# Second mixer: index key and index weights in one weight tile, seventeen tiles in place of eighteen

## What is computed

```python
q, k, v, qi, ki, wi = split(h @ w_in)          # 1024, 256, 256, 512, 64, 8 columns
q = _rope(_rmsnorm(q, q_norm_g), positions)
k = _rope(_rmsnorm(k, k_norm_g), positions)
qi = _rope(qi, positions)                      # 8 index heads of 64
ki = _rope(_layernorm(ki, idx_k_ln_g, idx_k_ln_b), positions)   # one index key head
wi = wi * (IDX_HEADS ** -0.5 * IDX_DIM ** -0.5)
# per block of 128 queries:
s = einsum('bqhd,bsd->bqhs', qib, ki)
score = einsum('bqhs,bqh->bqs', relu(s), wib)  # causal
_, sel = top_k(score, 128)                     # then attention over the selected keys
```

## Time and profile before

| | |
|---|---|
| time, median of 3 | 2121.99 us (2121.92 to 2122.03) |
| the profiled execution's own time | 2123.01 us |
| its span | 2120.9 us |
| PE, PEld busy | 99%, 81% |
| DVE, ACT, POOL busy | 58%, 37%, 14% |
| the chain that ended last | PE 91%, DVE 6%, ACT 1% |
| second mixer's tiles from index 3 to the attention | about 954 to 1063 us |
| its attention | about 1063 to 1171 us |

### The profile page before, as it was taken

One profiled execution on the slowest core, in us unless ns is written; L12 is line 12 of the kernel. 1 busy time (PEld: TensorE's weight loads), 2 busy tenths in 40 slices (PEclk: granted clock), 3 DMA queues, 4 the chain that ended last, 5 costly groups with the idle time before them and its releaser, 6 DMA issues.

```text
span 2120.9 us, 28344 instructions
## 1 busy us (share of the span) xinstructions
PE 2101.8 (99%) x10024; PEld 1725.9 (81%) x10024; DVE 1239.1 (58%) x1832; ACT 782.3 (37%) x1081; POOL 299.9 (14%) x357
## 2 busy tenths in 40 slices
PE   9999999999999999999999999999999999999999
PEld 8888888887888888877767788888888878888887
DVE  7666544786576654466995576654465456333332
ACT  6222333557432223344364432223343224222222
POOL 0122401650212240024300212210000000000000
PEclk9999999999999999999999999999999999999999
DMA  5566233320355632323300345542333222222232
GB/s 193 179 199 198 88 106 112 124 86 1 109 169 189 198 126 84 100 87 115 115 16 1 110 150 197 190 139 82 95 99 110 100 80 100 90 98 99 76 95 87
DMA packets 79572, 243.33 MB, mean 115 GB/s; under 512 B 12784, under 2 KB 13424, under 8 KB 79376
## 3 DMA queue, kind: packets, MB, share of 16 engines
q1 hardware_dynamic: 61376, 189.61, 27.3%
q0 software_dynamic: 18128, 52.84, 8.0%
HBM read 235.84 MB, written 2.29 MB: 112 GB/s over the span
## 4 chain that ended last, share of the span: by engine, by line
PE 91%; DVE 6%; ACT 1%; issue 1%; POOL 1%; DMA 0%; SPq 0%; ACTq 0%; DVEq 0%; POOLq 0%
PE ps L709 28%; PE ps L711 28%; PE ps L710 28%; PE ps L1016 2%; PE ps L974 1%; PE ps L995 1%; DVE tmp L1627 1%; DVE ps L1973 1%; DVE small L1868 1%; PE ps L977 0%; PE ps L1142 0%; DVE w_lo L1584 0%; ACT w_hi L1225 0%; POOL w_lo L618 0%; PE ps L743 0%
## 5 line engine op out<-in xcount | busy, mean ns | idle before, releaser
L709 PE MATMUL ps<-h_hi,w_hi 128*128 128x512 f32 x1888 | 740.1, 392 | 1.5 <-DVE h_lo L1913 0.9
L711 PE MATMUL ps<-h_hi,w_lo 128*128 128x512 f32 x1888 | 735.0, 389 | 0.0
L710 PE MATMUL ps<-h_lo,w_hi 128*128 128x512 f32 x1888 | 734.8, 389 | 0.0
L1584 DVE TENSOR_TENSOR w_lo<-w_raw,w_hi 128x1024 fp32r<-128x1024 f32 x336 | 411.4, 1226 | 381.3 <-ACT w_hi L1225 367.7
L1225 ACT ACTIVATE w_hi<-w_raw 128x1024 fp32r<-128x1024 f32 x383 | 402.2, 1052 | 242.0 <-PE ps L711 240.2
L709 PEld LDWEIGHTS ps<-h_hi,w_hi 128*128 128x128 f32 x1888 | 353.6, 187 | 82.2 <-issue 7.5
L711 PEld LDWEIGHTS ps<-h_hi,w_lo 128*128 128x128 f32 x1888 | 353.6, 187 | 75.2
L710 PEld LDWEIGHTS ps<-h_lo,w_hi 128*128 128x128 f32 x1888 | 353.7, 187 | 73.0 <-issue 0.2
L710 PE MATMUL ps<-hid_lo,w_hi 128*128 128x512 f32 x704 | 273.9, 389 | 0.0
L711 PE MATMUL ps<-hid_hi,w_lo 128*128 128x512 f32 x704 | 273.9, 389 | 0.0
L709 PE MATMUL ps<-hid_hi,w_hi 128*128 128x512 f32 x704 | 273.9, 389 | 0.0
(11 more groups left out here) (308 smaller groups left out, 1778.0 us busy)
## 6 DMA issues: line engine op xcount, KB each, us to landing
ada_raw<-in_ada_w POOLq DMA_DIRECT2D x96, 512.0 KB, 4.8
w_raw<-in_gate SPq DMA_DIRECT2D x88, 512.0 KB, 3.8
w_raw<-in_up SPq DMA_DIRECT2D x88, 512.0 KB, 3.5
w_raw<-in_down SPq DMA_DIRECT2D x64, 384.0 KB, 3.0
w_raw<-in_down SPq DMA_DIRECT2D x64, 320.0 KB, 2.8
w_raw<-in_w_mix_c SPq DMA_DIRECT2D x24, 512.0 KB, 3.4
w_raw<-in_w_mix_b SPq DMA_DIRECT2D x17, 512.0 KB, 3.5
w_raw<-in_w_mix SPq DMA_DIRECT2D x16, 512.0 KB, 3.5
```

What stands on the lines that cost most here:

```text
L709: pe.matmul(dest, s_hi, m_hi, start=first and n == 0, stop=False)
L710: pe.matmul(dest, s_hi, m_lo, start=False, stop=False)
L711: mm = pe.matmul(dest, s_lo, m_hi, start=False, stop=last and n == len(pairs) - 1)
L1584: dve.tensor_tensor(chunk(w_lo, slot, WT), chunk(w_raw, slot, WT), f32(chunk(w_hi, slot, WT)), ALU.subtract).then_inc(w_lo_done, 1)
```

## The change

The index key's 64 columns and the 8 index weights are put into one tile (the rest of it is zero), so there are seventeen tiles. The second tile of `first_two` is now `qi0`: DVE multiplies it by the rstd and ACT adds its shift. The key is made once, in the lower 64 partitions; a fifth DMA copies it to the upper ones, and the rope of the key waits for it. As the list is one shorter, what hangs on a tile's place moves: the loads with their swaps, POOL's waits, the ropes, the index slots (two chunks earlier), the rounds in `TOPS_AT` (32 early ones in place of 33), and the key's spread (from `betweenB(5, 0)` to `betweenB(4, 1)`).

```diff
                    "mk0", "mk1", "mv0", "mv1"]
-        TILES_B = ["ki", "wi", "qi0", "qi1", "qi2", "qi3", "vB0", "vB1", "kB0", "kB1"] + [f"qB{t}" for t in range(8)]
+        TILES_B = ["ki", "qi0", "qi1", "qi2", "qi3", "vB0", "vB1", "kB0", "kB1"] + [f"qB{t}" for t in range(8)]
         first_job, at = {}, 0
...
         def shift_sum(n, s):
-            return tmp[:, 3 * T + s * P:3 * T + s * P + (8 if n == 3 and s == 1 else P)]
+            return tmp[:, 3 * T + s * P:3 * T + (s + 1) * P]
 
...
             if t == "ki":
-                return 6
+                return 5
             at = (TILES_A if t in TILES_A else TILES_B).index(t)
...
                 return rot_ring[n % 2 + (0 if t in TILES_A else 2)], 64 * (n // 2 + 1)
-            return rot_key[t], 64
+            return rot_key[t], 80 if t == "ki" else 64
 
...
         ROUND_LIST = [(b, r) for b in range(1, TT) for r in range(ROUNDS)]
-        TOPS_AT = {8: (0, 1), 9: (4, 1), 10: (5, 2), 11: (4, 1), 12: (0, 2), 13: (3, 0), 14: (3, 0), 15: (3, 0), 16: (3, 0),
-                   17: (1, 0)}
+        TOPS_AT = {8: (1, 4), 9: (1, 5), 10: (2, 4), 11: (1, 0), 12: (2, 0), 13: (3, 0), 14: (3, 0), 15: (3, 0), 16: (3, 0)}
         TOP_EARLY = sum(before + between for before, between in TOPS_AT.values())
...
 
-            at = 4 * (m - 6) + 2 * part - 2
-            return IDX[max(at, 0):at + 2] if 0 <= at < len(IDX) else []
+            at = 4 * (m - 6) + 2 * part
+            return IDX[at:at + 2] if 0 <= at < len(IDX) else []
 
...
                         after(sp, h_sin, "ki")
+                if t == "ki":
+                    sp.dma_start(kraw[HD:P, :], kraw[0:HD, :]).then_inc(rot_sem(t)[0], 16)
                 half = 8 if t in TILES_A else HD // 2
                 for head in range(0, P, HD):
                     for to, of in ((head, head + half), (head + half, head)):
+                        of = of % HD if t == "ki" else of
                         sp.dma_start(turned(t)[to:to + half, :], straight(t)[of:of + half, :]).then_inc(rot_sem(t)[0], 16)
 
             def mixer(tiles, mix, last, weights):
                 J = first_job[mix]
                 for j in range(len(tiles) + KC):
                     if j < len(tiles):
-                        width = KC * 8 if tiles[j] == "wi" else WT
                         if tiles is TILES_B and j in (4, 5):
                             after(sp, shift_acc, (3, j - 4, KC - 1))
-                        load(J + j, 0, 4, A[weights][j, :, 0:width])
+                        load(J + j, 0, 4, A[weights][j])
                     else:
                         load(J + j, 0, 4, A[WEIGHTS[last]][j - len(tiles)])
-                    due = [t for t in tiles if has_rope(t) and j == tiles.index(t) + {"q": 7, "k": 10 if t == "ki" else 9}[t[0]]]
+                    due = [t for t in tiles if has_rope(t) and j == tiles.index(t) + {"q": 7, "k": 9}[t[0]]]
                     for t in sorted(due, key=lambda t: t[0] == "k"):
...
             for j in range(LEAD, len(TILES_B) + KC):
+                if j == 8:
+                    after(pool, h_roped, "qi3")
                 if j == 9:
-                    after(pool, h_roped, "qi3")
+                    after(pool, i_sum, (1, 5))
                 if j == 10:
-                    after(pool, i_sum, (1, 5))
-                if j == 11:
                     after(pool, i_sum, (2, 1))
-                if 15 <= j <= 20:
-                    after(pool, h_roped, f"qB{j - 15}")
+                if 14 <= j <= 19:
+                    after(pool, h_roped, f"qB{j - 14}")
                 split(first_job["mixB"] + j)
...
                         for s in range(2 * pair, 2 * pair + 2):
-                            width = 8 if n == 3 and s == 1 else P
-                            mm = product(None, bank(s)[0:width, :], [(weights(js + s, k, width),
-                                                                       (chunk(hi, k), chunk(lo, k)))], k == 0, k == KC - 1)
+                            mm = product(None, bank(s), [(weights(js + s, k), (chunk(hi, k), chunk(lo, k)))],
+                                         k == 0, k == KC - 1)
                             if k == KC - 1:
...
                 for b in range(MT if t[:2] == "mk" else TT):
-                    for half in range(2):
+                    for half in range(1 if t == "ki" else 2):
                         mm = pe.matmul(bank(5)[half * HD:(half + 1) * HD, b * P:(b + 1) * P],
...
                     after(pe, h_roped, "ki")
+                    after(pe, v_done, "wi")
                 if pair[0][0] == 1:
...
 
-                if part == 0 and m == 5:
+                if part == 1 and m == 4:
                     head_spread("ki")
-                if part == 0 and TILES_B[m - 2] in h_normed.value and m > 4:
+                if part == 0 and TILES_B[m - 2] in h_normed.value and m > 2:
                     head_spread(TILES_B[m - 2])
                 if part == 0 and m == 3:
                     after(pe, evac, "ki")
-                    pe.matmul(bank(6), matsB[:, P:2 * P], kraw[:, :], start=True, stop=True)\
+                    pe.matmul(bank(6)[0:HD, :], matsB[0:HD, P:P + HD], kraw[0:HD, :], start=True, stop=True)\
                         .then_inc(p_misc.at("ki_total"), 1)
                 if part == 1 and m == 3:
-                    turn_tile(TILES_B, 1)
-                if part == 0 and is_token_major(TILES_B[m - 1]) and m > 2:
-                    turn_tile(TILES_B, m - 1)
+                    turn_tile("wi")
+                if part == 0 and is_token_major(TILES_B[m - 1]):
+                    turn_tile(TILES_B[m - 1])
                 if part == 0 and has_norm(TILES_B[m - 1]):
...
             after(act, d_misc, "ki_scaled")
-            act.activation(kraw[:, :], kraw[:, :], ACT.Identity, bias=shift_out(3, 0)).then_inc(evac.at("ki"), 1)
+            act.activation(kraw[0:HD, :], kraw[0:HD, :], ACT.Identity, bias=shift_out(3, 0)[0:HD, :])\
+                .then_inc(evac.at("ki"), 1)
+            after(act, d_misc, "wi_scaled")
+            act.activation(features_of("wi"), features_of("wi"), ACT.Identity, bias=shift_out(3, 0)[HD:HD + 8, :])\
+                .then_inc(evac.at("wi"), 1)
             lead(J + 1)
             for m in range(2, len(TILES_B) + 1):
                 t = TILES_B[m - 1]
                 act.wait_ge(job_done, J + m + RING)
                 if has_norm(t):
                     head_square(t, hsB)
-                if t[:2] in ("qB", "qi"):
+                if t == "qi0":
+                    after(act, d_misc, "qi_scaled")
+                    act.activation(straight(t), straight(t), ACT.Identity, bias=shift_out(3, 1)).then_inc(h_scaled.at(t), 1)
+                elif t[:2] in ("qB", "qi"):
                     head_scale(t, col("g_q2") if t[:2] == "qB" else 1.0, straight(t))
                 elif t[:2] == "kB":
                     head_gain(t, col("g_k2"), straight(t))
-                elif t == "wi":
-                    after(act, d_misc, "wi_scaled")
-                    act.activation(features_of(t), features_of(t), ACT.Identity, bias=shift_out(3, 1)[0:8, :])\
-                        .then_inc(evac.at(t), 1)
                 else:
                     act.activation(features_of(t), tile_bank(t), ACT.Copy).then_inc(evac.at(t), 1)
                 if m < len(TILES_B):
                     lead(J + m)
                 if m == 3:
                     after(act, d_misc, "ki_ctr")
-                    head_square("ki", hsB, src=kraw[:, :])
+                    head_square("ki", hsB, src=kraw[0:HD, :])
                 if m == 3:
-                    keep_tile("wi", 1, wi[:, :], WI_SCALE)
+                    keep_tile("wi", 0, wi[:, :], WI_SCALE)
                 if t[:2] == "vB":
...
                 after_nth(dve, h_roped, before)
+                if t == "ki":
+                    dve.wait_ge(*rot_sem(t))
                 dve.tensor_tensor(chunk(rop, 0), straight(t), tab_cos, ALU.mult)
...
             dve.wait_ge(job_done, J + 2 + RING)
-            dve.tensor_tensor(kraw[:, :], bank(0), ssum[:, :], ALU.mult).then_inc(d_misc.at("ki_scaled"), 1)
-            dve.tensor_tensor(relu[0:8, 0:T], bank(1)[0:8, :], ssum[0:8, :], ALU.mult).then_inc(d_misc.at("wi_scaled"), 1)
+            dve.tensor_tensor(kraw[0:HD, :], bank(0)[0:HD, :], ssum[0:HD, :], ALU.mult).then_inc(d_misc.at("ki_scaled"), 1)
+            dve.tensor_tensor(features_of("wi"), bank(0)[HD:HD + 8, :], ssum[HD:HD + 8, :], ALU.mult)\
+                .then_inc(d_misc.at("wi_scaled"), 1)
+            dve.tensor_tensor(straight("qi0"), bank(1), ssum[:, :], ALU.mult).then_inc(d_misc.at("qi_scaled"), 1)
 
...
                     after(dve, p_misc, "ki_total")
-                    dve.scalar_tensor_tensor(kraw[:, :], bank(6), -1.0 / HD, kraw[:, :], ALU.mult, ALU.add)\
+                    dve.scalar_tensor_tensor(kraw[0:HD, :], bank(6)[0:HD, :], -1.0 / HD, kraw[0:HD, :], ALU.mult, ALU.add)\
```

(11 more changed lines are left out.)

40 lines of the change are left out of this document (20 added, 20 removed).

## The result

After the change the kernel takes 2136.77 us (median of 6 runs, 2132.67 to 2145.39), and the kernel before, run beside it, 2123.39 us (6 runs, 2121.92 to 2126.48). The ratio is 1.0062, with a 95% interval of 1.0047 to 1.0077. Slower was predicted; 2130.7 us was not, and 2136.77 lies 2.8 us above the range. The profiled execution took 2137.41 us, its span is 2135.6 us.

A forecast was written before the change was run, and what follows sets the result against it. PE (99% busy) was taken to bound the kernel, with helpers it waits for: -5.95 + 0.75 + 5.4 + 1.65 + 1.5 + 2.15 + 2.9 + 0.3 = +8.7 us, giving a median of 2130.7 us; range 2121 to 2134.

The forecast's parts named there:

- The tile: Second mixer: one tile less on PE saves 5.44 us, the key's smaller rstd spread 0.5: gain 5.95 us.
- The start: Stage's start: PE waits longer for DVE's shift sum, now 128 columns wide: +0.75 us, bounds 0.5 and 1.1.
- Stall A: At the index key's spread PE waits for DVE's reciprocal behind qi1's rope: +5.4 us, lower bound 3.4.
- Stall B: At the turn of vB1 PE waits for ScalarE's evacuation behind relu 3: +1.65 us, range 0.6 to 1.7.
- rival (c): PE's clock halves after a stall, hidden after A, not after E: +1.4 us; chance of over 2134 us 0.07.
- C: Index loop, kB0's spread: its rstd comes behind sums 10, 11 and four rounds: +1.5 us, range 0.3 to 1.5.
- D: Index loop, kB1's spread: its rstd comes late behind five rounds on DVE: +2.15 us, bounds 1.5 and 2.5.
- E: Index loop, qB2's head sum: its squares wait behind relus 22, 23, sums and ropes: +2.9 us, lower 1.2.
- The attention: Its first scores wait for DVE, which ends the tile loop about 0.3 us further behind PE: +0.3 us.

The follow-up runs named there:

- e12: e10 with DVE's ropes of kB0 and kB1 behind the sums of their step, two rounds moved behind them, one fewer in the loop; 2126.94 us, 1.0001.
- e11: The kernel before with its second tile 128 columns wide, 8 of them used (wide load, sum and matmuls); 2127.28 us, ratio 1.0018.
- e5: The changed kernel with small unread matmuls ahead of the waits at the spreads of the key, kB0 and kB1; 2134.85 us, ratio 1.0052.
- e2: The changed kernel with the index key's std on ACT and its reciprocal on DVE taken earlier; 2137.26 us, ratio 1.0065.
- e4: The changed kernel with only DVE's reciprocals of kB0 and kB1 earlier, ahead of the second slot's rounds and sums; 2134.60 us, ratio 1.0059.
- e7: e3 and e4 joined, plus DVE's norms of kB0 and kB1 ahead of the second slot's rounds; 2132.05 us, ratio 1.0043.
- e1: The changed kernel with only the key's spread put back to its old place, chunk 2 of tile 5; 2137.49 us, ratio 1.0057.
- e3: e2 plus DVE's norm of the key ahead of the rope of qi1, so its swap comes earlier; 2130.47 us, ratio 1.0036.
- e8: The changed kernel with the index slots and the distribution of rounds as before the change, nothing else; 2135.37 us, ratio 1.0049.
- e9: e7 with the index slots and rounds as before the change; 2128.85 us, ratio 1.0020.
- e10: e9 with PE's product of the shift sums moved behind the stage's first six matmuls; 2127.30 us, ratio 1.0009.
- e13: e12 with small unread matmuls: 3 ahead of the last head sum, 9 in place of 5 behind the attention's second scores; 2123.94 us, 1.0001.
- e14: The kernel before with only PE's product of the shift sums moved behind the stage's first six matmuls; 2122.48 us, ratio 0.9989.

## Why the prediction was right in sign and too small

- **The tile, -5.95: 1.0 too much.** e12's loop is 5.4 us shorter than before's with no new wait in it, 0.4 of it from the start; so the change is worth 5.0. The pitch of the tile, 5.44, was right, but the spread of the key's rstd is no shorter for having 8 matmuls in place of 16: 1.02 us from its start to the next matmul in e12, and 1.03 before. The key's sum, now made in 64 partitions only, keeps PE for 1.00 us in place of 0.46. The first fence is before, the second e12:

```profile
954.64 1.02 PE L1153 MATMUL ps<-kraw,matsB 128*128 128x512 f32 x2
955.10 0.80 PE L709 MATMUL ps<-h_hi,w_hi 128*128 128x512 f32 x1
...
969.02 0.50 PE L709 MATMUL ps<-h_hi,w_hi 128*128 128x512 f32 x1
```
```profile
955.28 1.07 PE L1165 MATMUL ps<-kraw,matsB 64*64 64x512 f32 x2
956.28 0.50 PE L712 MATMUL ps<-h_hi,w_hi 128*128 128x512 f32 x1
...
965.78 1.09 PE L956 MATMUL ps<-identity,hrB 128*64 128x128 f32 x8
966.80 0.50 PE L712 MATMUL ps<-h_hi,w_hi 128*128 128x512 f32 x1
```

- **The start, +0.75:** +0.93, right. Its second effect was not in the sum: behind the longer wait the clock falls in part of the traces (e11: 3.1 us on the mean span, not 0.9).
- **Stall A, +5.4: right,** place, releaser and size (5.0 listed, 5.1 net of a matmul's pitch). The collision with GpSimd is in the row of 1.78 us for the product with the sine, started at 969.07 while GpSimd's split ran from 967.82 to 970.30. The Trainium skill (SBUF — State Buffer, "Who interferes with whom") says that a DVE instruction with two SBUF inputs contends with a GpSimd one that reads SBUF; this row, 1.78 us against 0.69 for the same shape alone, agrees.
- **Stall B, +1.65:** 0.3 to 0.5, as rival (c) said: PE ran slowly between A and B. It is 0.9 with full clock in e5 and 1.6 in e2, so the working was near, but it took PE to be at full clock between A and B.
- **C, +1.5:** 1.1 to 1.3. **D, +2.15:** 2.8; only its upper bound of 2.5 was off. I had it behind DVE's reciprocal alone. e4 shows a second condition, the norm of kB0, that would have held it just as long.
- **E, +2.9: not there,** because PE lost more at D and in the slow clock behind it than E needs. It was real: 3.3 us as soon as D was cured (e7). That the waits are counted from PE's own last step, "so a stall ahead of it does not pay for it", was the wrong sentence, for DVE is the one that is late, and while PE waits or runs slowly at D, DVE catches up.
- **The attention, +0.3:** 0.3 in the profile (1061.50 to 1170.30 before, 1072.63 to 1181.77 after, 108.8 and 109.1). For the changed kernel right, but e12 shows that DVE has no room there.
- **The sum** of what was found is -4.9 + 0.93 + 5.1 + 0.5 + 1.3 + 2.9 + 0.3 = 6.1, and at full clock 5.9 was measured. The prediction's sum of waits and tile, 8.7, was 2.8 us too large: E was counted and not there, B was smaller, and the tile was overrated, which goes the other way. With the clock of before, the time would have been 2128 to 2129, inside the range; that two of these errors partly cancel is luck. (The sum of all upper bounds is 9.45 and not 9.8, which moves the upper end by 0.4 us and decides nothing.)
- **The step that failed is rival (c), the clock.** The sum put the clock at nothing, and the rival priced it at 1.4 us, or 4.3 if it hit twice, with a chance of 0.07 for more than 2134: after A hidden by B, after E not. Measured: 7.5 us on the mean. In the profile it follows A (3.4 us of half clock) and D (6.8 us, of which 3.4 are lost), and comes behind the mixer as well; in profiles of other kernels here it comes also at the stage's start (e1, e2, e3, e7, e11) and at the attention's start (17 to 20 us in e8, e9, e10 and e12). That A's stretch is mostly hidden by B was right (B lost 1.2 us of wait). D's was not foreseen, and behind the mixer, where the rival looked for none, this profile loses another 3.4 us (1224 and 1773). The 10.7 us of new waits (the start, A, B, C and D) came with 7.5 of clock, and e5, by filling three of them, took 5.7 of it off. The Trainium skill (TensorE: Matmul & The Clock Gate, "HAM oscillation — how this bites in real kernels") says that waits inside a matmul stream can drop the clock again and again, so that what follows a wait starts slowly; the rows behind A and D agree. By that rule the prediction had estimated the sum at +10 to +12; the median is 13.4 above the before beside it. The rule deserved the larger chance.

**Open:** why stretches at half the clock come more often far behind the mixer (6.8 us at 1224 in place of 3.4, and 3.4 at 1773 in place of none; the one at 1722 stands in before too, at 1708), where the code is unchanged and only runs 11 to 14 us later. e11 has others (1161, 1765), and half of its runs have a clock as high as before's usual one. No run here tells that apart. Since they vary from run to run, only medians over many runs show them, and e12 against e13 stays unsettled for the same reason.

## What to carry to other kernels

When an engine on the critical path loses a piece of work, every helper must be that much earlier; ask of each helper's written list not whether it has idle time on average but what stands ahead of the item that is wanted. Cure one late item and the next is what you measure: A, D, E and the attention's third scores came up in that order, and the loop showed the whole of the saved tile only when A, C, D, E and most of the start's wait were cured together (e12). On PE, price each new wait of a microsecond or more inside a matmul stream at more than its length (here 10.7 us of them came with 7.5 of clock besides), and compare kernels over many runs with the granted clock beside each span.

## What the runs showed of the hardware

- Stretches at half the clock followed each wait of 4.7 to 5.0 us at the key's spread (four traces) and each of 2.8 us at kB1's spread (seven traces), but only five of eleven waits of 1.8 to 2.1 us at the stage's start, and not the wait of 2.4 us at qB2's head sum in e9. They were 3.4 us long at least, and 17 to 20 us at the attention's start in e8, e9, e10 and e12, where PE has waits and matmuls of few columns together; before has none there in its trace.
- Half as many small matmuls did not make the spread shorter: 8 into 64 partitions take 1.02 us, and 16 into both halves 1.03.
- Small matmuls that nobody reads, put into a wait, kept the clock in the one profile taken: none of the 3.4 and 6.8 us behind A and D was left in e5, while 3.4 us stood behind the wait without them.
- Taking the shift product out of PE's way at the start of the stage (e14) went with 1.0 us less at full clock (2116.4 to 2115.4), for a wait of 1.2.
